# Attention half of a layer: query factor moved into the exponential, mask added by TensorE, taps taken off GpSimd, a new order of TensorE's work

## What is computed

```python
h = rmsnorm(x, norm_mix[l])
proj = einsum('btd,de->bte', h, w_in[l])             # 512 tokens, 1024 -> 4352 columns
q, k, v, u, ug, ga, gb = split(proj)                 # 16 query heads of 64, 2 key heads
q = partial_rope(rmsnorm(q, q_norm[l]), cos, sin)    # norm over the 64 of a head
k = partial_rope(rmsnorm(k, k_norm[l]), cos, sin)
# sliding window of 128 keys, in blocks of 128 queries and 256 keys
s = einsum('bnqkgd,bnskd->bnkgqs', qb, kb) * HEAD_DIM ** -0.5
s = where(mask, s, -inf)
m = maximum(max(s), sink)
p = exp(s - m); p = p / (sum(p) + exp(sink - m))
a_out = einsum('bnkgqs,bnskd->bnqkgd', p, vb)
a = u * sigmoid(ug)                                  # conformer branch
y = depthwise_conv(a, w_dw, width=31) + b_dw         # 512 channels, 31 taps
c_out = silu(layernorm(y)) @ w_pw
merged = sigmoid(ga) * a_out + sigmoid(gb) * c_out
x = x + merged @ w_out[l]
```

## Time and profile before

| | us |
|---|---|
| median of 3 runs | 2447.99 (2447.51 to 2448.48) |
| the profiled execution | 2443.4 |
| its span, first to last instruction | 2441.6 |
| mean granted TensorE clock | 0.976 of full |
| first product to first conformer output product, layer 1 of 2 | 9.71 to 321.93 |
| the same, layer 2 of 2 | 751.88 to 1055.74 |

### The profile page before, as it was taken

One profiled execution on the slowest core, in us unless ns is written; L12 is line 12 of the kernel. 1 busy time (PEld: TensorE's weight loads), 2 busy tenths in 40 slices (PEclk: granted clock), 3 DMA queues, 4 the chain that ended last, 5 costly groups with the idle time before them and its releaser, 6 DMA issues.

```text
span 2441.6 us, 30010 instructions
## 1 busy us (share of the span) xinstructions
PE 2299.9 (94%) x10648; PEld 1883.4 (77%) x10648; DVE 1509.2 (62%) x2054; ACT 1003.0 (41%) x1297; POOL 287.0 (12%) x189
## 2 busy tenths in 40 slices
PE   7888999999999888999999998999999996999996
PEld 5676778888887667778888888888887784888885
DVE  7889974444435889975444334653676456888723
ACT  3567554443222567554443223323334424333221
POOL 1354101000001344101000000000000013000010
PEclk9999999999999999999999999989999997999998
DMA  4110122222223211122222233212222221222221
GB/s 160 69 53 35 55 84 104 102 87 98 83 95 114 70 52 36 52 87 104 92 97 98 76 102 113 87 68 83 98 70 79 77 88 50 95 94 103 77 96 69
DMA packets 32642, 204.40 MB, mean 84 GB/s; under 512 B 3616, under 2 KB 4000, under 8 KB 13344
## 3 DMA queue, kind: packets, MB, share of 16 engines
q1 hardware_dynamic: 32544, 203.13, 23.6%
HBM read 201.02 MB, written 2.10 MB: 83 GB/s over the span
## 4 chain that ended last, share of the span: by engine, by line
PE 69%; issue 14%; DVE 9%; POOL 5%; ACT 2%; DMA 0%; POOLq 0%; DVEq 0%; SPq 0%; ACTq 0%
PE mm L1417 22%; PE mm L1418 22%; PE mm L1419 22%; POOL conv_y L399 3%; DVE w_lo L886 1%; POOL sq L384 1%; PE misc L1440 1%; DVE probs L1045 1%; DVE conv_y L956 1%; ACT w_hi L458 1%; DVE probs L1065 1%; POOL sq L387 0%; DVE x L1347 0%; DVE pt_lo L1009 0%; PE ob L1417 0%
## 5 line engine op out<-in xcount | busy, mean ns | idle before, releaser
L1417 PE MATMUL mm<-in_hi,w_hi 128*128 128x512 f32 x1984 | 803.7, 405 | 39.0 <-DVE in_lo L915 17.6
L1418 PE MATMUL mm<-in_lo,w_hi 128*128 128x512 f32 x1984 | 778.5, 392 | 0.0
L1419 PE MATMUL mm<-in_hi,w_lo 128*128 128x512 f32 x1984 | 777.6, 392 | 0.0
L458 ACT ACTIVATE w_hi<-w_raw 128x2048 fp32r<-128x2048 f32 (+2 forms) x202 | 355.1, 1758 | 676.1 <-PE mm L1419 672.5
L886 DVE TENSOR_TENSOR w_lo<-w_raw,w_hi 128x2048 fp32r<-128x2048 f32 (+2 forms) x205 | 456.0, 2225 | 214.4 <-ACT w_hi L458 213.8
L1417 PEld LDWEIGHTS mm<-in_hi,w_hi 128*128 128x128 f32 x1984 | 376.3, 190 | 142.0 <-issue 31.1
L1418 PEld LDWEIGHTS mm<-in_lo,w_hi 128*128 128x128 f32 x1984 | 376.6, 190 | 87.8 <-issue 12.4
L1419 PEld LDWEIGHTS mm<-in_hi,w_lo 128*128 128x128 f32 x1984 | 376.1, 190 | 79.6
L379 POOL TENSOR_TENSOR ssum<-ssum,sq 128x512 f32<-128x512 f32 x56 | 93.4, 1668 | 1835.8 <-ACT sq L475 1835.7
L1417 PE MATMUL mm<-act_hi,w_hi 128*128 128x512 f32 x528 | 205.4, 389 | 0.0
L1418 PE MATMUL mm<-act_lo,w_hi 128*128 128x512 f32 x528 | 205.4, 389 | 0.0
(11 more groups left out here) (332 smaller groups left out, 3033.5 us busy)
## 6 DMA issues: line engine op xcount, KB each, us to landing
w_raw<-in_w_dram SPq DMA_DIRECT2D x149, 1024.0 KB, 4.7
w_raw<-in_w_dram SPq DMA_DIRECT2D x48, 704.0 KB, 3.9
w_raw<-in_w_dram SPq DMA_DIRECT2D x6, 512.0 KB, 3.6
out_dram<-x SPq DMA_DIRECT2D x8, 256.0 KB, 2.0
rope<-in_rope_dram SPq DMA_DIRECT2D x3, 512.0 KB, 3.9
...
```

Of the source, the lines that this page charges most:

```text
L458: e.activation(whi[:, slot, 0:cols], raw[:, slot, 0:cols], ACT.Copy).then_inc(s_whi, whi_out.up())
L1417: MM(out, ah, bh, start=first, stop=False, **kw)
L1418: MM(out, ah, bl, start=False, stop=False, **kw)
L1419: return MM(out, al, bh, start=False, stop=last, **kw)
```

## The change

Query: ScalarE squares the raw tile and copies it times the weight `q_norm` to SBUF (`raw_query`); the rotation is applied to this raw query, and the norm factor, one number for a token and a head, is kept apart in `q_scale` (128x8). Its mean comes from `head_sums` (four small float32 products with two columns), its root from ScalarE and four GpSimd instructions on 128x8 (`q_scale`). It enters as the per-partition scale of the exponential and multiplies the row maxima. The mask enters through TensorE: the unit matrix times the mask starts each accumulation of scores. Maxima are plain reductions from PSUM; the exponential reads PSUM and writes `probs`; ScalarE, not VectorE, divides the probabilities (`normalise`). All 124 taps are VectorE's, none GpSimd's. The scores of both heads alternate product by product. Sums over channel tiles for the layer norm are four accumulating float32 products each on TensorE instead of three additions on VectorE each.

Order: the chunks now come as u0, u1, key, value, u2, u3, and the loop over `c` has eight turns, with the scores of pair `c` at the end of its own chunk, so that the softmax of pair `c` meets the transposes in the middle of chunk `c+1`. The `gb` chunks follow after it.

```diff
-TAPS_U, TAPS_KV = (8, 8, 8, 8), 6
-TAPS_ATT = (6, 5) + (QT - 2) * (4,) + (14, 6)
-VT = CT - 1
-assert sum(TAPS_U) + TAPS_KV + sum(TAPS_ATT) == VT * TAPS
+TAPS_U, TAPS_KV = ((8, 0), (8, 0), (4, 4), (4, 3)), 6
+TAPS_Q = ((2, 2, 7),) + (QT - 1) * ((2, 2, 4),)
+TAPS_B = (8, 5, 7)
+assert sum(map(sum, TAPS_U)) + TAPS_KV + sum(map(sum, TAPS_Q)) + sum(TAPS_B) == CT * TAPS
...
+            def q_scale():
+
+                mean, r, t = (qs[:, j, :] for j in range(3))
+                e.wait_ge(s_qx, guess.next())
+                e.tensor_tensor(t, r, r, ALU.mult).then_inc(s_po, own.up())
+                e.wait_ge(s_po, own.now())
+                e.tensor_tensor(t, t, mean, ALU.mult).then_inc(s_po, own.up())
+                e.wait_ge(s_po, own.now())
+                L.park(s_idle)
+                e.tensor_scalar(t, t, -0.5, 1.5, ALU.mult, ALU.add).then_inc(s_po, own.up())
+                e.wait_ge(s_po, own.now())
+                e.tensor_tensor(r, r, t, ALU.mult).then_inc(s_qn, scale.up())
...
+            def exps(s, h):
+
+                e.wait_ge(s_m, mxs.next())
+                head = 2 * s + h
+                hs = slice(4 * h, 4 * h + 4)
+                e.activation(es[:, hs], ng[:, hs], ACT.Exp, bias=parl[:, A_SINK + head:A_SINK + head + 1])
+                for n in range(TB):
+                    w0 = P if n == 0 else 0
+                    j = 4 * h + n
+                    last = e.activation(pr[:, h, n, w0:256], sp[h][:, n, w0:256], ACT.Exp, scale=qs[:, 1, j:j + 1],
+                                        bias=ng[:, j:j + 1], accum_out=ls[:, j:j + 1])
+                last.then_inc(s_e, ex.up())
...
+            def normalise(h):
+
+                e.wait_ge(s_rl, dens.next())
+                for n in range(TB):
+                    p = pr[:, h, n, (P if n == 0 else 0):256]
+                    last = e.activation(p, p, ACT.Copy, scale=rl[:, 4 * h + n:4 * h + n + 1])
+                last.then_inc(s_p, probs.up())
...
+            def raw_query():
+
+                e.wait_ge(s_mm, tiles.next())
+                e.activation(sq[:, 0, :], mm[0][:], ACT.Square).then_inc(s_sqq, sqq.up())
+                e.activation(ssum[:], mm[0][:], ACT.Copy, scale=parl[:, A_QN:A_QN + 1]).then_inc(s_qr, raw_q.up())
...
+                for c in range(QT):
+                    if c:
+                        exps(c - 1, 0)
+                        exps(c - 1, 1)
+                        normalise(0)
+                    raw_query()
+                    if c:
+                        normalise(1)
+                        pt_hi(0)
+                    scale_guess()
+                    if c:
+                        pt_hi(1)
+                    misc_taken.skip(1)
+                    e.wait_ge(s_val, val.next())
+                    hi(qh[:, c % 2, :], tD[:])
+                    tiles.skip(1)
+                    prep(c % 2)
...
+                def softmax_max(s, h):
+                    e.wait_ge(s_s, scores.next())
+                    if h == 0:
+                        e.wait_ge(s_qn, scale.next())
+                    hs = slice(4 * h, 4 * h + 4)
+                    sink = parl[:, A_SINK + 2 * s + h:A_SINK + 2 * s + h + 1]
+                    e.tensor_reduce(mx[:, 4 * h:4 * h + 1], sp[h][:, 0:1, P:256], mybir.AxisListType.X, ALU.max)
+                    step(e.tensor_reduce(mx[:, 4 * h + 1:4 * h + 4], sp[h][:, 1:TB, :], mybir.AxisListType.X, ALU.max))
+                    step(TT(mx[:, hs], mx[:, hs], qs[:, 1, hs], ALU.mult))
+                    TS(ng[:, hs], mx[:, hs], sink, -1.0, ALU.max, ALU.mult).then_inc(s_m, mxs.up())
+
+                def denominator(h):
+                    e.wait_ge(s_e, ex.next())
+                    hs = slice(4 * h, 4 * h + 4)
+                    step(TT(ls[:, hs], ls[:, hs], es[:, hs], ALU.add))
+                    e.reciprocal(rl[:, hs], ls[:, hs]).then_inc(s_rl, dens.up())
+
...
+                e.wait_ge(s_do, own.now())
+                take_up()
+                e.wait_ge(s_o, o_in.next())
+                TS(rt[:], ob[:, 0:TB], HD * EPS / D, HD * EPS * EPS, ALU.mult, ALU.add).then_inc(s_of, o_taken.up())
+                up_gate(0)
+                convolve(TAPS_U[0][0])
+                prep(0, CH // 2)
+                take_up()
+                up_gate(1)
+                convolve(TAPS_U[1][0])
+                prep(1, CH // 2)
+
                 e.wait_ge(s_mm, tiles.next())
                 e.tensor_copy(kraw, mm[0][:]).then_inc(s_mmf, taken.up())
+                convolve(TAPS_KV)
+                take(vval, 1)
                 prep(0)
-                take(vval, 1)
                 e.wait_ge(s_ms, misc.next())
-                step(STT(tB[:, 0:T], ems[:], HD * EPS, mi[:], ALU.mult, ALU.add))
-                TS(tB[:, 0:T], tB[:, 0:T], 1.0 / HD, None, ALU.mult).then_inc(s_msf, misc_taken.up())
-                convolve(TAPS_KV)
+                step(STT(kt, ems, HD * EPS, mi[:], ALU.mult, ALU.add))
+                TS(kt, kt, 1.0 / HD, None, ALU.mult).then_inc(s_msf, misc_taken.up())
+                take_up()
+                prep(1)
                 e.wait_ge(s_root, root.next())
-                STT(kraw, kraw, parl[:, A_KN:A_KN + 1], tC[:], ALU.mult, ALU.mult).then_inc(s_rot, rot.up())
-
-                before = (4,) * QT + (8, TAPS_ATT[QT + 1])
-                for c in range(QT + 2):
-                    if c < QT:
...
+                for c in range(QT):
+                    if c:
+                        softmax_max(c - 1, 0)
+                        softmax_max(c - 1, 1)
+                    if c > 1:
+                        gate_heads(c - 2)
+                    convolve(TAPS_Q[c][0])
+                    if c:
+                        denominator(0)
+                    convolve(TAPS_Q[c][1])
+                    if c:
+                        denominator(1)
+                    prep((c + 1) % 2)
+                    tiles.skip(1)
+                    e.wait_ge(s_qr, raw_q.next())
+                    TT(tB[:, 0:T], ssum[:], rope1[:, 0, :], ALU.mult).then_inc(s_mmf, taken.up())
+                    e.wait_ge(s_hs, sums.next())
+                    TT(qs[:, 0, :].rearrange("p (h b) -> p h b", h=2),
+                       ob[:, 0:8].rearrange("p (b h) -> p h b", h=2),
+                       rt[:, :].rearrange("p (a b) -> p a b", a=1).broadcast_to([P, 2, TB]),
+                       ALU.add).then_inc(s_hm, means.up())
+                    e.wait_ge(s_ms, misc.next())
+                    TT(tC[:], mi[:], rope1[:, 1, :], ALU.mult).then_inc(s_msf, misc_taken.up())
+                    e.wait_ge(s_mmf, taken.now())
+                    e.wait_ge(s_msf, misc_taken.now())
+                    if c:
+                        e.wait_ge(s_q, qo.now())
+                    TT(tD[:], tB[:, 0:T], tC[:], ALU.add).then_inc(s_val, val.up())
+                    if c:
+                        pt_lo(0)
+                    lo(ql[:, c % 2, :], tD[:], qh[:, c % 2, :], qo)
+                    if c:
+                        pt_lo(1)
+                    take(ga[:, c, :], 1)
+                    convolve(TAPS_Q[c][2])
...
+            def attend(s):
+
+                heads = (slice(0, 64), slice(64, 128))
+                if s == 0:
+                    e.wait_ge(s_em, em_in.next())
+                    e.wait_ge(s_kv, kv_in.next(2))
+                twice = mask[:, P:384].rearrange("p (a b) -> p a b", a=1).broadcast_to([P, 2, 256])
+                for h in range(2):
+                    if s and h:
+                        e.wait_ge(s_ptl, ptlo.next())
+                    MM(spf[h][:, P:T], eye, mask, start=True, stop=False, skip_group_check=True)
+                    MM(sp[h][:, 2:4, :], eye, twice, start=True, stop=False, skip_group_check=True)
+                e.wait_ge(s_q, q_in.next())
                 for n in range(TB):
-                    k0 = max(n - 1, 0) * P
-                    qs = slice(n * P, (n + 1) * P)
-                    ks = slice(k0, (n + 1) * P)
-                    ins = mm3(sp[h][:, n, (P if n == 0 else 0):256], qh[a, s % 2, qs], ql[a, s % 2, qs],
-                              kh[a, s // 4, ks], kl[a, s // 4, ks], True, True)
-                ins.then_inc(s_s, scores.up())
+                    w0 = P if n == 0 else 0
+                    qt = slice(n * P, (n + 1) * P)
+                    kb = slice(max(n - 1, 0) * P, (n + 1) * P)
+                    for q, k, last in ((qh, kh, False), (qh, kl, False), (ql, kh, True)):
+                        for h, a in enumerate(heads):
+                            ins = MM(sp[h][:, n, w0:256], q[a, s % 2, qt], k[a, s // 4, kb], start=False,
+                                     stop=last, skip_group_check=True)
+                            if last and n == TB - 1:
+                                ins.then_inc(s_s, scores.up())
...
+            def head_sums():
+
+                e.wait_ge(s_sqq, sqq.next())
+                for b in range(TB):
```

(54 more changed lines are left out.)

432 lines of the change are left out of this document (176 added, 256 removed).

## The result

The changed kernel takes 2407.9 us in the median (2406.6 to 2410.0) against 2447.8 (2442.0 to 2448.5): a ratio of 0.9843, 95% interval 0.9826 to 0.986. The forecast was 2414. Its profiled execution has a span of 2404.8 us, 36.8 less than before.

A forecast was written before the change was run, and what follows sets the result against it. VectorE was taken to bound the loop before, TensorE after, at 20.0 us a turn. 2443.4 less 21.8 and 19.1 for the layers, plus 6.8 for clock falls, gave 2409.3 profiled; median 4.6 higher, 2414, range 2380 to 2455.

The forecast's parts named there:

- The turn: One pass of the query-tile loop: bound moves to TensorE, 19.5 us of work, taken as 20.0, against 23.3 before.
- crossings: Allowance in each loop turn for waits between engines: 0.5 us on top of TensorE's 19.5.
- The chain: In a loop turn, from scores through maxima, exponentials and divisions to TensorE's transposes: 7.2 us.
- cover: TensorE reaches the transposes 9.5 us after the scores, 2.3 us more than the softmax needs.
- rival D: Softmax from scores to transposes takes 12.5 us, TensorE waits 3.2 a turn: 2476 us in all, chance 0.12.
- a fall of the clock: TensorE's clock drops from 2.4 to 1.2 GHz after a wait, costing 3.4 us; one charged per layer, 6.8 in all.
- The start: Each layer before the query loop: TensorE waits 4.7 and 2.8 us for `w_lo` and 3.9 for the scaled key.
- turn 0: First query tile of the first layer's loop: its scores end at 104.3 us.
- Turn 1: Second query tile: 22.5 us, as VectorE still owes seven taps and is 3 us beyond its cover.
- The tail: After the loop, up to the conformer's output: 53.3 us, so that output starts at 300.1 in the first layer.
- The sum: Whole profiled execution: 2443.4 less 21.8 and 19.1 for the two layers, plus 6.8 for clock falls, 2409.3 us.
- Why GpSimd matters: GpSimd's SBUF reads stretch VectorE's taps to a loop mean of 1156 ns; without GpSimd a tap costs 0.75 us.

The follow-up runs named there:

- delay runs: Changed kernel with three or six 128x512 ScalarE copies added between the row maxima and the first exponential of each turn: 2420.6 us and 2472.2 us.
- six copies: Changed kernel with six 128x512 in-place ScalarE copies between the row maxima and the first exponential of each turn: 2472.2 us, 1.011 of before.
- the run without the fourth group: Kernel before, leaving out 30 of the 31 taps of the fourth channel group, so no GpSimd additions or ScalarE tap products: 2411.8 us, 0.9869 of before.

## Why the prediction was right, and where it was not

**The turn** was forecast at 20.0 with 19.5 of TensorE work and is 19.66. Term by term: scores 1.60 (1.6), product with the values 2.82 (2.9), head sums 0.81 (0.9), rotation with its return 0.94 (0.9); only the masks are 0.96 instead of 0.8. The 0.5 for crossings was not needed: every crossing is covered.

**VectorE** works 17.0 us a turn (103.5 / 120 x 19.66), below my 17.5 to 19.0. The tap is 0.744 (0.75), the two reductions of a head together 0.95 + 0.29 = 1.24 (1.08), the two small instructions behind them 0.16 + 0.23 = 0.39 (0.35). **ScalarE** has 15.1 (15.6); its division is at 0.53 what I bounded by an exponential's 0.494, and the exponential from PSUM takes 0.566 on the same rows.

**The chain**: 7.8 us from the scores to the divided probabilities (forecast 7.2), cover 1.9 (2.3). The delay runs give rival D its price: it was real, 2 us away, and a fall of the clock behind most of its waits is what six copies show. (D's own sum has a slip: 12.5 less the cover of 9.5 is a wait of 3.0, not 3.2, so 3 us less than 2476.)

**The start**: waits of 4.35, 2.2 and 3.7 us for forecasts of 4.7, 2.8 and 3.9, and putting VectorE's list in another order took them away. Even so turn 0 ends at 107.2, not 104.3: the window from 40 to 92 has a clock of 0.90, so 52 x 0.10 / 0.5 = 10 us at the lower level, half of it lost. **Turn 1** was the worst term of the layer: 25.7 from the end of turn 0's scores to the end of its own product with the values, for 22.5. I had counted the seven taps that VectorE owes (TensorE waits 2.8) but not that the clock falls right behind: the window from 104 to 126 has 0.84, so 22 x 0.16 / 0.5 = 7.0 us at the lower level, half of it lost. The tail took 55.0 for 53.3, in the main since the four products of a channel sum start 0.86 us apart (the last takes 0.45), where I had 0.46 each, two passes of 0.23:

```profile
291.60 1.02 PE L1616 MATMUL misc<-tA,cst 128*128 128x512 f32 x2
292.45 1.02 PE L1616 MATMUL misc<-tC,cst 128*128 128x512 f32 x2
```

So the first layer's conformer output begins at 305.9, not 300.1; against before the two layers gain 16.0 and, from their own first product (733.3 against 751.9), 14.5, where I had 21.8 and 19.1.

**The sum came out by luck closer than its terms.** My stages stood at the full clock, so the 21.8 and 19.1 count the old falls as gone, and I charged 6.8 us for new ones. The old ones, as the earlier trace rows, are gone with the loop's waits, but the new ones in the start and turn 1 are as long: the lower level stands for 17 us in the first layer and 14 in the second, as before. That costs 15.4 us at half speed, 8.6 more than I charged. Against that, the stages without their falls are 2.7 and 2.2 us shorter than forecast, and the stage of the conformer output, which I left out, is 2.8 us shorter in each layer (23.6 against 26.4). The sum for the profiled execution was 2409.3, measured are 2406.6.

**Why GpSimd matters** was right in its rule and wrong in the part that I blamed. A tap is at 0.75 once GpSimd is out, yet the run without the fourth group shows that in the loop its additions hardly touched the taps: the root did. The additions cost the division, `w_lo` and the waits through ScalarE's list. None of the parts that I tried makes the gain: paired scores alone give nothing, taps on VectorE alone nothing, and the division's move nothing. My reading is that three have to come together: the query's factor on eight columns (which takes the root off GpSimd and two full-size instructions off VectorE), the cheaper maxima, and the taps. It is argued, not shown: no run has the factor without the maxima, and none has the new order of the chunks and of TensorE's turn without the rest, so what each of these is worth stays open.
